# Eleven input weight tiles move into the chunked recurrence of a two-block decoder kernel

## The reference

```python
h = rms_norm(x, norm_in_g[l])
p = h @ w_in[l]
p_rwkv, p_nsa, p_mem = jnp.split(p, [RWKV_COLS, RWKV_COLS + NSA_COLS], axis=-1)
y_rwkv = rwkv7_group(p_rwkv, ...)      # shift by one token, then a scan over the 512 tokens
y_nsa = nsa_group(p_nsa, ...)          # needs its columns of p only after the scan's stage here
y_mem = memory_group(p_mem, mem_k, mem_v, ...)
```

## Time and profile before

| | us |
|---|---|
| median of 3 runs | 2059.31 (2058.52 to 2062.81) |
| the profiled execution, its own time | 2064.54 |
| its span, first to last instruction | 2062.4 |
| TensorE busy | 1891.5 (92% of the span) |
| VectorE, ScalarE, GpSimd busy | 936.0, 843.1, 252.2 |
| input stage, dense part (46.5 to 199.0) | 152.5 |
| recurrence (259.5 to 427.4) | 167.9 |

### The profile page before, as it was taken

One profiled execution on the slowest core, in us unless ns is written; L12 is line 12 of the kernel. 1 busy time (PEld: TensorE's weight loads), 2 busy tenths in 40 slices (PEclk: granted clock), 3 DMA queues, 4 the chain that ended last, 5 costly groups with the idle time before them and its releaser, 6 DMA issues. The chain is left out here.

```text
span 2062.4 us, 31831 instructions
## 1 busy us (share of the span) xinstructions
PE 1891.5 (92%) x12732; PEld 1529.4 (74%) x12732; DVE 936.0 (45%) x1622; ACT 843.1 (41%) x1361; POOL 252.2 (12%) x209
## 2 busy tenths in 40 slices
PE   6999389969979889989999999999999899999997
PEld 5888088847757657668788888878887778888886
DVE  2343935463355677745333333265554443333333
ACT  4322334434533443543443432275654343444222
POOL 3000223220003220002100000032221020000000
PEclk9999659869989989999999999999999899999998
DMA  4331010010012100002233333222221213232321
GB/s 169 98 92 56 0 43 3 3 45 1 1 42 67 56 26 1 1 21 82 79 95 97 97 95 99 92 77 72 72 74 41 67 57 102 92 102 92 102 92 51
DMA packets 37763, 131.71 MB, mean 64 GB/s; under 512 B 4816, under 2 KB 5136, under 8 KB 37392
## 3 DMA queue, kind: packets, MB, share of 16 engines
q1 hardware_dynamic: 36784, 127.91, 19.9%
q10 hardware_dynamic: 864, 2.17, 0.3%
HBM read 127.17 MB, written 2.10 MB: 63 GB/s over the span
## 5 line engine op out<-in xcount | busy, mean ns | idle before, releaser
L138 DVE TENSOR_TENSOR big_parts<-ring,big_parts 128x1024 fp32r<-128x1024 f32 x164 | 204.8, 1250 | 526.9 <-ACT big_parts L133 526.9
L156 PE MATMUL bank<-h_parts,big_parts 128*128 128x512 f32 x960 | 381.4, 397 | 10.2 <-DVE big_parts L138 6.5
L157 PE MATMUL bank<-y_parts,big_parts 128*128 128x512 f32 x960 | 375.9, 392 | 0.0
L158 PE MATMUL bank<-h_parts,big_parts 128*128 128x512 f32 x960 | 375.6, 391 | 0.0
L133 ACT ACTIVATE big_parts<-ring 128x1024 fp32r<-128x1024 f32 x164 | 173.7, 1061 | 285.6 <-PE bank L158 285.4
L156 PEld LDWEIGHTS bank<-h_parts,big_parts 128*128 128x128 f32 x960 | 181.2, 189 | 56.6 <-issue 12.5
L158 PEld LDWEIGHTS bank<-h_parts,big_parts 128*128 128x128 f32 x960 | 181.5, 189 | 38.5
L157 PEld LDWEIGHTS bank<-y_parts,big_parts 128*128 128x128 f32 x960 | 181.6, 189 | 36.2
L157 PE MATMUL bank<-y_parts,work_parts 128*128 128x512 f32 x456 | 180.2, 395 | 0.0
L138 DVE TENSOR_TENSOR work_parts<-ring,work_parts 128x1024 fp32r<-128x1024 f32 x65 | 79.3, 1223 | 166.8 <-ACT work_parts L133 166.8
L133 ACT ACTIVATE work_parts<-ring 128x1024 fp32r<-128x1024 f32 x65 | 68.7, 1060 | 175.9 <-PE bank L158 175.9
(11 more groups left out here) (404 smaller groups left out, 2999.7 us busy)
## 6 DMA issues: line engine op xcount, KB each, us to landing
ring<-in_wstream SPq DMA_DIRECT2D x229, 512.0 KB, 3.6
x<-in_xt SPq DMA_DIRECT2D x4, 512.0 KB, 8.1
out_t<-x SPq DMA_DIRECT2D x8, 256.0 KB, 2.0
work<-in_memt ACTq DMA_DIRECT2D x1, 1024.0 KB, 15.2
work<-in_cw SPq DMA_DIRECT2D x1, 1024.0 KB, 5.3
cst<-in_cst ACTq DMA_DIRECT2D x1, 704.0 KB, 7.9
cos<-in_reset SPq DMA_DIRECT2D x2, 256.0 KB, 3.3
big<-work SPq DMA_DIRECT2D x4, 128.0 KB, 3.8
```

What stands on the lines that cost most here:

```text
L138: dve.tensor_tensor(self.parts[:, self.place_of(n), 1, :, :], self.ring[:, n % RING, :, :], self.parts[:, self.place_of(n), 0, :, :].bitca ...
L156: pe.matmul(out, w[0], x[0], start=start, stop=False, skip_group_check=True)
L157: pe.matmul(out, w[0], x[1], start=False, stop=False, skip_group_check=True)
L158: return pe.matmul(out, w[1], x[0], start=False, stop=stop, skip_group_check=True)
```

## The change

The 11 tiles of the attention groups leave `stage_in` and are made in `stage_rwkv_chunks`. They are multiplied there as plain fp32, straight from the ring, without cast and split: 8 products 128x128 by 512 a tile, 88 in all, summed in a PSUM bank of their own (bank 5), so that the recurrence's groups rotate over five banks. The order is cut into its 50 levels (`rwkv_levels`). Tile j begins in level 9j//2 and has four levels with two products each: one behind the first group of the level and one behind the last. Levels 8, 17, 26, 35, 44 and 49 have none. At the start of the level behind its fourth, ScalarE waits for the tile and copies it out in two halves; these counts also free the ring's place and the bank.

Around it: the stream has the order RWKV tiles, memory, attention tiles (`ns`); the first four `ns` slabs are loaded in `stage_in`, the others and the four of the next dense stage in the recurrence. The normalised input is written over `c.x` (in the recurrence `c.h` is used for other data), and `stage_middle` loads the input again, in four DMAs of 512 KB. In `stage_in` the memory's statistics, root, normalisation and cast are spread over the RWKV tiles: the 8 squares products stand behind the fourth tile, the root behind tile 5, and memory tiles are normalised and cast one for each tile.

```diff
-    for name, n in (("in", IN_TILES), ("mem", 4), ("out", MIX_TILES), ("att", ATT_TILES), ("uq", UQ_TILES // 4),
+    for name, n in (("in", RW_TILES), ("mem", 4), ("ns", NS_TILES), ("out", MIX_TILES), ("att", ATT_TILES), ("uq", UQ_TILES // 4),
...
+    def raw_slab(self, n, k):
+
+        return self.ring[:, n % RING, k, :]
+
+    def raw_wait(self, pe, n):
+
+        pe.wait_ge(self.slab_ready[n % RING], 16 * (n // RING + 1))
+
...
-    hp = TileParts(c, "in_h", c.h, wkr(c, 15 * T, KT, T), c.yr)
+    hp = TileParts(c, "in_h", c.x, wkr(c, 15 * T, KT, T), c.yr)
...
-            c.load_slabs(sp, 0, n_mem + 4)
+            c.load_slabs(sp, 0, n_mem + 4 + RING)
...
+            for t in range(RW_TILES):
+                c.slab_done_wait(act, n_in + t)
+                c.cast_slab(act, n_in + t + PARTS)
+                act.activation(c.big[:, t, :], c.bank[t % RING][:, :], ACT.Copy, scale=c.omu[:, t:t + 1]).then_inc(scaled, 1)
+                if t == 4:
+                    act.wait_ge(stats, 1)
+                    act.activation(root_m, c.bank[6][:, 0:M], ACT.Sqrt, bias=c.eps[:, 0:1], scale=1.0 / D).then_inc(roots, 1)
+                if 7 <= t < 7 + KT:
+                    act.wait_ge(memh_ready, t - 6)
+                    mem.scalar(act, t - 7)
...
-            for lo, hi in ((1, PR_WA // RING), (PR_WA // RING, IN_TILES // RING)):
-                if lo > 1:
-                    for k in range(KT):
-                        pe.wait_ge(squares, k + 1)
-                        mm = pe.matmul(c.bank[6][:, 0:M], con(c, "ones"), squares_m[:, k, :], start=k == 0, stop=k == KT - 1)
-                    mm.then_inc(stats, 1)
-                with pe.Fori(lo, hi) as i:
-                    for u in range(RING):
-                        pe.wait_ge(free[u], i)
-                        tile(u, i)
+            for k in range(KT):
+                pe.wait_ge(squares, k + 1)
+                mm = pe.matmul(c.bank[6][:, 0:M], con(c, "ones"), squares_m[:, k, :], start=k == 0, stop=k == KT - 1)
+            mm.then_inc(stats, 1)
+            with pe.Fori(1, PR_WA // RING) as i:
+                for u in range(RING):
+                    pe.wait_ge(free[u], i)
+                    tile(u, i)
...
-            for t in range(PR_WA + 1, IN_TILES):
+            for t in range(RW_TILES):
                 c.split_slab(dve, n_in + t + PARTS)
-                c.slab_done_wait(dve, n_in + t)
-                dve.tensor_copy(c.big[:, t, :], c.bank[t % RING][:, :]).then_inc(free[t % RING], 1)
-                if t == PR_WA + 1:
...
+DENSE_BANK = 5
+PAIRS = KT // 2
+
+
+def first_level(j):
+
+    return 9 * j // 2
 
...
+    part_at = {first_level(j) + p: (j, p) for j in range(NS_TILES) for p in range(PAIRS)}
+    out_level = {first_level(j) + PAIRS: j for j in range(NS_TILES)}
...
-            b = sum(1 for k2 in turn if k2[0] not in ("uy", "y")) % 6
+            b = sum(1 for k2 in turn if k2[0] not in ("uy", "y")) % DENSE_BANK
...
-            c.load_slabs(sp, PLAN["out"], PLAN["out"] + RING)
+            c.load_slabs(sp, n_ns + RING, PLAN["out"] + RING)
...
+            def dense(j, p, x):
+
+                n, k = n_ns + j, 2 * p + x
+                if k == 0:
+                    c.raw_wait(pe, n)
+                    if j:
+                        c.slab_done_wait(pe, n - 1)
+                mm = pe.matmul(c.bank[DENSE_BANK][:, :], c.raw_slab(n, k), c.x[:, k, :], start=k == 0, stop=k == KT - 1)
+                if k == KT - 1:
+                    mm.then_inc(c.slab_split, 1)
...
+            for lv, level in enumerate(levels):
+                for key in level[:1]:
+                    step(key)
+                if lv in part_at:
+                    dense(*part_at[lv], 0)
+                for key in level[1:]:
+                    step(key)
+                if lv in part_at:
+                    dense(*part_at[lv], 1)
...
+            def dense_out(j):
+
+                n, t = n_ns + j, RW_TILES + j
+                c.slab_wait(act, n)
+                act.activation(c.big[:, t, 0:M], c.bank[DENSE_BANK][:, 0:M], ACT.Copy).then_inc(c.slab_cast, 1)
+                act.activation(c.big[:, t, M:T], c.bank[DENSE_BANK][:, M:T], ACT.Copy).then_inc(c.slab_done, 1)
+
+            for lv, level in enumerate(levels):
+                if lv in out_level:
+                    dense_out(out_level[lv])
+                for key in level:
+                    step(key)
...
+            for i in range(KT // 2):
+                sp.dma_start(c.x[:, 2 * i:2 * i + 2, :], a["xt"][:, 2 * i:2 * i + 2, :]).then_inc(x_loaded, 16)
```

More of the change, by code:

```diff
@@ L356, in _ @@
                 c.cast_slab(act, n_mem + PARTS + j)
-                act.activation(c.km[:, j, :], c.bank[j][:, 0:M], ACT.Copy)
+                act.activation(c.km[:, j, :], c.bank[1 + j][:, 0:M], ACT.Copy)
             act.wait_ge(gl_out, 1)
@@ L412, in _ @@
                     for half in HALVES:
-                        mm = pe.matmul(c.bank[4][half, 12 * q:12 * q + 12], c.h[:, k, q * P:(q + 1) * P][:, half], c.wgl[:, k, :],
+                        mm = pe.matmul(c.bank[4][half, 12 * q:12 * q + 12], c.x[:, k, q * P:(q + 1) * P][:, half], c.wgl[:, k, :],
                                        start=k == 0, stop=k == KT - 1)
@@ L418, in _ @@
                 c.slab_wait(pe, n_mem + 2 + j)
[L419 removed]
+            pe.wait_ge(free[3], PR_WA // RING)
+            pe.wait_ge(free[0], PR_WA // RING + 1)
             for j in range(2):
@@ L423, in _ @@
                     w = [c.parts[:, s, a, 2 * (k % 4):2 * (k % 4) + 2, :].rearrange("p a b -> p (a b)") for a in range(2)]
-                    mm = product(pe, c.bank[2 + j][:, 0:M], [t[:, j * P:(j + 1) * P] for t in mem.tile(k)], w,
+                    mm = product(pe, c.bank[(3 + j) % RING][:, 0:M], [t[:, j * P:(j + 1) * P] for t in mem.tile(k)], w,
                                  k == 0, k == KT - 1)
@@ L449, in _ @@
-            with dve.Fori(0, 4) as i:
-                for u in range(RING):
-                    c.split_slab(dve, n_in + u + PARTS, i)
-                    dve.wait_ge(scaled, i * RING + (u + 1))
-                    shift(i * RING + u, u, c.vecs[:, bass.ds(i * RING + (u + VECS["mu"]), 1)])
-            c.split_slab(dve, n_in + PR_WA + PARTS)
-            dve.wait_ge(scaled, 17)
-            shift(PR_WA, 0, vec(c, "mu", 16))
-            dve.wait_ge(roots, 1)
-            dve.reciprocal(root_m, root_m).then_inc(inverses, 1)
@@ L604, in rwkv_steps @@
     state = [("uy",), ("sa",), ("y", "st"), ("yt",), ()]
-    steps = []
+    levels = []
     for s in range(NCH + 2):
         for lv in range(5):
+            levels.append([])
             for names, ch in ((first[lv], s), (rest[lv], s - 1), (state[lv], s - 2)):
                 if 0 <= ch < NCH:
-                    steps += [(n, ch) for n in names if not (n == "st" and ch == NCH - 1)]
-    return steps
+                    levels[-1] += [(n, ch) for n in names if not (n == "st" and ch == NCH - 1)]
+    return levels
+DENSE_BANK = 5
+PAIRS = KT // 2
+def first_level(j):
+    return 9 * j // 2
 def stage_rwkv_chunks(c):
@@ L630, in stage_rwkv_chunks @@
     pcb = c.pcb
-    steps = rwkv_steps()
+    levels = rwkv_levels()
+    steps = [key for level in levels for key in level]
+    n_ns = PLAN["ns"]
+    part_at = {first_level(j) + p: (j, p) for j in range(NS_TILES) for p in range(PAIRS)}
+    out_level = {first_level(j) + PAIRS: j for j in range(NS_TILES)}
     by_dve = ("ga", "gb", "ma", "mb", "r2", "r3", "r4", "xt", "v1", "w", "sa", "st", "yt")
@@ L690, in each, with step @@
                 return mm
-            for key in steps:
+            def dense(j, p, x):
[7 more added lines that the diff above has]
+                    mm.then_inc(c.slab_split, 1)
+            def step(key):
                 name, ch = key
```

69 lines of the change are left out of this document (31 added, 38 removed).

## The result

| | before | changed |
|---|---|---|
| time, median of 6 executions of each | 2058.91 us | 2080.39 us |
| ratio, with its 95% interval | | 1.0082 (1.0052 to 1.0113) |
| the profiled execution: time, span | 2064.5, 2062.4 us | 2079.83, 2077.7 us |
| its mean granted clock | 0.937 | 0.949 |

The change makes the kernel about 1% slower: 0.8% by the ratio, which is of mean times and leaves out the slow execution of 2104.97 us, and 1.0% by the two medians. The six changed executions took 2072.7, 2079.83, 2079.89, 2080.89, 2082.56 and 2104.97 us; their mean granted clocks fall as the times rise, from 0.952 to 0.935.

What follows compares the result with a forecast made beforehand. TensorE was taken to fill the input stage at full clock and nearly fill the recurrence, partly at half clock. -59.8 + 59.3 + 1.5 = +1.0 us on the profiled 2064.5, less 5.2 to the median: 2060, range 2045 to 2078.

Steps and rivals of the forecast that it cites:

- The likeliest case: Whole kernel: removed and added terms nearly cancel, a change under 0.2%; 2052 to 2068 us, chance 0.43.
- rival 3: Recurrence: ScalarE's single-bank copy and delayed gb stretch each of ten turns by 1.2 us; 2072 us, chance 0.22.
- What leaves the input stage: Input stage: eleven tiles of 24 split products, 5.44 us each, go from TensorE; 59.8 us off.
- rival 5: Input stage: moved memory work delays splits, so the 59.8 us are not given; +10, 2070 us, chance 0.02.
- 88 products: Recurrence, TensorE: 88 plain fp32 products, 128x128 by 512, at 0.86 us each add 75.7 us.
- Excursions: Recurrence: 70 shape changes from 64x64 tiles to 128x128 and back, 0.32 us each, add 22.4 us.
- Rival 2: Recurrence: a shape change and back costs 0.16 us, or remaining waits go too; 2045 to 2050 us, chance 0.27.
- Waits: Recurrence, TensorE: the wait before p1 goes in the full turns; what is left over sums to 9.0 us.
- The clock: Recurrence: half clock costs 3.5 us at the start, a fall in turns 1 and 2 costs 2; otherwise 1.00.
- rival 4: Recurrence: the clock stays at half in turns 1 to 3, 9 and 10; about 2115 us, chance 0.06.
- Recurrence: Whole recurrence stage: 114.6 + 75.7 + 22.4 + 9.0 + 5.5 = 227.2 us, against 167.9: +59.3.
- Middle stage: Middle stage: slabs issued ahead of its eight loads delay GpSimd's first products; +1.5 us (0 to 3).

Runs made afterwards that it cites:

- experiment 4: Changed kernel with both products of a level behind its last group: 2046.08 us, ratio 0.9935 to the kernel before; on another chip 2044.63 us, 0.991.
- experiment 7: Kernel before with its recurrence's groups over five banks instead of six, nothing else: 2059.62 us, ratio 1.0005.
- experiment 3: Changed kernel with four 256-column dummy products in the wait before p1 of turn 2 alone: ratio 1.0052 to the kernel before.
- experiment 9: Experiment 4's kernel with the next dense stage's last slab loaded behind the middle stage's constants: 2046.8 us, ratio 0.9943.
- experiment 10: Experiment 9's kernel plus three dummy products behind each rk product in the stage ahead of the recurrence: 2047.95 us, ratio 0.9935.
- experiment 1: Changed kernel with 5, 4 and 2 dummy products ahead of p1 of chunks 0, 1 and 2: 2065.39 us, ratio 1.0022 to the kernel before.
- experiment 5: Changed kernel with both products of a level behind its first group: 2079.06 us, ratio 1.0106 to the kernel before.
- experiments 7 and 8: Experiment 7, and the kernel before with two or three dummy products in eight waits of the first and last turns: 2064.46 us, ratio 1.0021.

## Why the prediction was right, and where it was off

The time lies 20 us above the 2060 given. The median of all six executions is 2.4 us above the range's 2078; the ratio, 1.0082 of 2059.3, gives 2076.2, just within it. The direction with the highest chance came, but at 0.37 for slower against 0.36 for faster that is luck. The likeliest case, no change worth the name, did not come, and rival 3, whose time (2072) is the nearest, is wrong in its mechanism. By its own steps:

- **What leaves the input stage**: 59.8 forecast, 60.1 measured, at the same 5.44 us a tile. The cover by ScalarE and VectorE held; rival 5 is out.
- **88 products**: 0.86 forecast; in a pair the second adds 0.85 to the first (1.81 from 314.88 to 316.69 in experiment 4, less 0.96 for a single one), and with 0.86 the turns of experiment 4 come out to 0.1 us.
- **Excursions**: 0.32 forecast, 0.36 measured (0.33 to 0.39 by the turns 4 to 6 of the kernels above): 70 x 0.04 is 2.8 us more. Rival 2 (0.16) is out. The Trainium skill, "TensorEngine Tiling (Array Packing)", "Key Properties", has that a change of tiling mode drains TensorE. These turns agree: the cost goes with the number of changes of shape (two, three or eight a turn), not with the number of products.
- **Waits**: none before p1 in turns 4 to 7, as forecast; 2.2, 1.5, 0.7 and 0.8 us left in turns 1, 2, 3 and 8, where 2.0, 1.7, 0.7 and 1.3 had been taken. Rival 3, 1.2 us more in each turn, is out: turns 4 and 5 take 24.2 and 26.52, within 0.2 us of their sum of terms. Five banks: nothing (experiment 7).
- **The clock**: this is the step that failed in size. "I add 2 us for a fall in turns 1 and 2, where waits stay." The fall came in turns 2 and 3 and cost 12.0 us (60.25 less 48.3). The premise behind it, "What the stretch lacks is wide products", fell too: from 232.7 to 260.0 there were wide products at every level but one, and the clock stayed at 0.50 for 27.3 us. The trace of before speaks against it as well, for its half clock ended at 302.8 in work as narrow as that ahead of it; the window behind the stretch of the earlier trace rows:

```profile
302.80:313.10 10.30, 9.90 (x266) 9.37 (x264) 5.51 (x13) 6.54 (x17) 2.42 (x5) 1.00 0.01 3
```

  That the fall comes with waits that stay was right; that it costs 2 us was not. The sign named for rival 4, wide products at half clock past the first turn, did show, in turns 2 and 3 (2.00 us with its change of shape, 235.41 to 237.41 is such a step, against 1.06 at the full clock), but from turn 4 on the clock was 1.00, so the rival's 2115 did not follow.
- **Recurrence**: 227.2 forecast, 240.0 measured. 12.0 less the 2 that were taken, and 2.8: 12.8. Without the fall, in experiment 3's profiled execution, it is 228.2 us, 1.0 from the forecast.
- **Middle stage**: +1.5 forecast (0 to 3), +2.5 measured. The cause named, the late slab, is neither borne out by experiment 9 (10.4 us) nor ruled out by experiment 10 (8.2), and the constants' time varies between executions without the change too (7.9 to 9.3). The cause stays open.
- **Not foreseen**: 1.7 us in a later attention stage, which the change doesn't touch (88.4 to 86.7). It was 86.6 in experiment 4 and 88.5 in its repetition, so it goes with the execution; why is open.
- **From the profile to the median**: the profiled execution came out 14.3 us above its forecast of 2065.5: 12.8 of the recurrence, 1.0 of the middle stage, 1.7 of the attention stage, the rest small and the other way. The other 5.8 us of the miss are the step from the profiled execution to the median. Before's profile lay 5.2 above its median, and that was carried over; the changed one's lies 0.6 below its own.

The Trainium skill, "TensorE: Matmul & The Clock Gate", "Why this matters for your kernels", which the prediction weighed against a busy stretch at half clock, says to keep TensorE busy without idle gaps. The changed kernel disagrees in the same way as before: busy for 27.10 of 27.30 us, at 0.50. But its other side, that gaps are to be avoided, agrees with experiment 1: the upper group of times is empty in 12 executions once the gaps are filled.

In one sentence: the change takes away 60.1 us of split products and about 41 us of waits and half clock (168.0 less 114.6, against 228.2 less 114.6, 75.7 and 25.2), and puts in 75.7 us of plain products and 25.2 us of changes of shape. That cancels; the middle stage adds 2.5, and a fall that comes in most executions adds 12. What can be had back lies in where the first product of each pair stands: moved behind the last group, the same work makes the kernel 0.65% faster than before (0.9% on the second chip).

## What to carry to other kernels

Work put into the gaps of a stage is priced as pieces times (duration + change of tile shape), and where the stage has no wait left the price is plain addition; so put it in few large pieces, behind a group that has its shape already, and behind what other engines wait for, never in front of it. A remaining wait of 1.5 to 2 us in TensorE is worth little for its own length here, and much for the clock fall of 12 us that may follow it; count the falls that may come, not those that the trace happens to show, and look at single executions for two groups of times. Dummies in such waits took the long fall away in all of 12 executions at no cost that shows, but moving the real work so that the waits shrink gave more.

## What was not expected of the hardware

- After a wait of 1.49 us and 1.7 us of work, the granted clock stood at 0.50 from 232.7 to 260.0 with TensorE busy 99% of the time, 128x128 by 512 products among it. The same wait (1.48 us) in another execution was followed by none of this. Of the seven falls in the profiled recurrences of kernels with the change, five begin in or within 2 us behind a wait of 1.49 us or more; the other two (at 253.5 in experiment 5, at 238.7 in experiment 10) have only waits of 0.2 to 0.6 us in the 10 us ahead of them. What decides is open.
- The first products that need the middle stage's constants started 7.9, 8.5 and 9.3 us into it in three profiled executions of kernels without the change (before, experiments 7 and 8), and 8.2 to 11.5 us in eleven with it, without a clear relation to what was queued ahead of or behind them.
